# Rotating queries and keys with small transfers in place of a matrix product, on VectorE in another order

## The reference

```
h = modulate(x, norm_mix_g[l], shift1, scale1)      # shifts and scales from c_act @ w_ada + b_ada
proj = h @ w_in[l]                                  # pooled input, q, k, v, gates
q = rope_partial(qkv[0], pos)
k = rope_partial(qkv[1], pos)
attn = moba_attention(q, k, qkv[2])                 # 8 heads of 64
x = x + gate1 * (merged @ w_out[l])
x = x + gate2 * peer_ffn(modulate(x, ...), ...)     # 16 experts for each of 8 heads, by top-k

def rope_partial(x, pos):                           # half = 8 features
    x1, x2, rest = x[..., :half], x[..., half:16], x[..., 16:]
    return concatenate([x1 * cos - x2 * sin, x1 * sin + x2 * cos, rest], axis=-1)
```

## Time and profile before

| what | value |
|---|---|
| median of 3 runs | 1173.78 us (1173.57 to 1175.6) |
| the profiled execution | 1174.26 us, of which the span is 1172.4 us |
| PE busy | 1041.2 us, 89% |
| DVE busy | 826.7 us, 71% |
| ACT busy | 423.2 us, 36% |
| POOL busy | 290.3 us, 25% |
| chain that ended last | PE 52%, DMA 31%, DVE 11%, ACT 3% of the span |

### The profile page before, as it was taken

One profiled execution on the slowest core, in us unless ns is written; L12 is line 12 of the kernel. 1 busy time (PEld: TensorE's weight loads), 2 busy tenths in 40 slices (PEclk: granted clock), 3 DMA queues, 4 the chain that ended last, 5 costly groups with the idle time before them and its releaser, 6 DMA issues.

```text
span 1172.4 us, 13740 instructions
## 1 busy us (share of the span) xinstructions
PE 1041.2 (89%) x5066; PEld 702.4 (60%) x5066; DVE 826.7 (71%) x1912; ACT 423.2 (36%) x895; POOL 290.3 (25%) x262
## 2 busy tenths in 40 slices
PE   5999999898999996886886878788899999999997
PEld 3799976644555543432332323333389878999986
DVE  5699765768767768778887555555566878888843
ACT  3545622322332222222222111111266665665631
POOL 0000001444354543353544444445000000000000
PEclk8999999999999998898988999989999999999999
DMA  9977594999999999899999999999994443554530
GB/s 367 427 319 297 239 399 158 418 401 422 420 419 420 421 422 421 365 410 421 422 421 421 422 421 422 420 422 422 384 396 180 145 179 134 198 209 163 197 144 37
DMA packets 48199, 390.46 MB, mean 333 GB/s; under 512 B 5498, under 2 KB 5890, under 8 KB 7300
## 3 DMA queue, kind: packets, MB, share of 16 engines
q0 software_dynamic: 37040, 269.51, 55.5%
q1 hardware_dynamic: 11092, 120.07, 26.1%
HBM read 388.50 MB, written 1.06 MB: 332 GB/s over the span
## 4 chain that ended last, share of the span: by engine, by line
PE 52%; DMA 31%; DVE 11%; ACT 3%; issue 2%; POOL 1%; SPq 1%; DVEq 0%
DMA ring<-in_uv,idx 27%; PE ps L1457 18%; PE ps L1801 15%; PE ps L1958 5%; DMA ring<-in_w_ada 4%; DVE ring L1243 3%; PE ps L1669 2%; PE ps L1611 2%; PE ps L1886 2%; PE ps L1481 1%; PE ps L1684 1%; DVE ring_r L885 1%; POOL ring L514 1%; PE ps L1510 1%; DVE ring L896 1%
## 5 line engine op out<-in xcount | busy, mean ns | idle before, releaser
L1801 PE MATMUL ps<-ring,probT 128*128 128x512 f32 x1020 | 490.7, 625 | 103.6 <-ACT probT L759 102.1
L1243 DVE CUSTOM_DVE_ANT_0 ring<-h2t,ring 128x1024 f32<-128x1024 f32 x255 | 308.7, 1222 | 166.0 <-DMA ring<-in_uv,idx 165.8
L1801 PEld LDWEIGHTS ps<-ring,probT 128*128 128x128 f32 x1020 | 192.6, 199 | 338.8 <-issue 194.7
L514 POOL DMA_INDIRECT ring<-in_uv,idx x255 | 287.9, 1129 | 339.1 <-PE ps L1801 287.0
L1457 PE MATMUL ps<-util_r,ring_r 128*128 128x256 f32 x1312 | 216.9, 282 | 0.0
L1457 PEld LDWEIGHTS ps<-util_r,ring_r 128*128 128x128 f32 x1312 | 181.6, 189 | 1.3 <-issue 1.1
L885 DVE TENSOR_TENSOR ring_r<-ring,ring_r 128x1024 fp32r<-128x1024 f32 x134 | 157.7, 1220 | 34.0 <-ACT ring_r L536 33.9
L754 ACT ACTIVATE prob<-prob 128x2 f32<-128x2 f32 (+2 forms) x98 | 20.0, 204 | 368.5 <-DVE prob L1243 368.4
L536 ACT ACTIVATE ring_r<-ring 128x1024 fp32r<-128x1024 f32 x134 | 133.6, 1050 | 41.5 <-DMA ring<-in_w_in 19.3
L1457 PE MATMUL ps<-h_r,ring_r 128*128 128x256 f32 x704 | 126.1, 282 | 0.1
L759 ACT ACTIVATE probT<-ct,prob 128x128 f32<-128x128 f32 x256 | 85.5, 392 | 76.5 <-DVE prob L1249 75.8
(11 more groups left out here) (213 smaller groups left out, 980.4 us busy)
## 6 DMA issues: line engine op xcount, KB each, us to landing
ring<-in_w_in SPq DMA_DIRECT2D x12, 2048.0 KB, 13.8
ring<-in_w_up SPq DMA_DIRECT2D x11, 2048.0 KB, 7.9
ring<-in_w_ada SPq DMA_DIRECT2D x7, 2048.0 KB, 9.8
ring<-in_w_down SPq DMA_DIRECT2D x6, 2048.0 KB, 7.7
ring<-in_w_ada SPq DMA_DIRECT2D x8, 1024.0 KB, 16.4
ring<-in_w_out SPq DMA_DIRECT2D x4, 2048.0 KB, 8.0
ring<-in_w_q SPq DMA_DIRECT2D x3, 2048.0 KB, 11.3
ring<-in_w_br SPq DMA_DIRECT2D x2, 2048.0 KB, 13.1
```

Of the source, the lines that this page charges most:

```text
L514: e.indirect_dma_start(out=row_buf[n], out_offset=None, in_=uv, in_offset=bass.IndirectOffsetOnAxis(ap=idx[:, tt, k:k + 1], axis=0)).then_inc(
L1243: e.tensor_tensor_reduce(u, h2t[:, tt, :], u, 1.0, 0.0, ALU.mult, ALU.add, av[:, tt, n % 128:n % 128 + 1]).then_inc(*made.put(("dot", n)))
L1801: ins = e.matmul(acc[half][:, :], diag[:, n % 8, :], row_buf[n][:, D + half * 512:D + (half + 1) * 512], start=(k == 0), stop=(k == 127))
```

## The change

The matrix product goes. Instead GpSimd clears both scratch tiles, and as soon as ScalarE has copied all of the queries it issues four transfers within SBUF, each of 8 partitions x 1024 elements (32 KB), from `qT` into the scratch tile, with the groups of partitions exchanged. For the keys it does the same after their copy. VectorE's first pass now multiplies the scratch tile by `sinm` in place, whose sign moves from `rot` into the constant. The partitions that no transfer writes stay zero.

On VectorE the order of calls changes. The low parts of quarters 12 to 15 and `ada(6)` come ahead of the queries' rotation, the keys' rotation comes ahead of quarters 18 and 19, and `ada(5)` moves behind `normed` of heads 0 and 1, where `ada(7)` follows it directly. The order of the loads on SyncE is as it was.

```diff
--- before.py
+++ after.py
@@ -360,13 +360,15 @@
         arrived_in = {b: Mark(sem(f"s_rows{b[0]}{b[1]}"), 16) for b in bufs}
         arrived = [arrived_in[b] for b, _ in ROW_BUFS]
         spread_sums = Mark(sem("s_sums"), 16)
+        swapped = {name: Mark(sem(f"s_swapped_{name}"), 16) for name in ("q", "k")}
+        cleared = Mark(sem("s_cleared"))
         stored = Mark(sem("s_stored"), 16)
         high = Mark(sem("s_high"))
         low = Mark(sem("s_low"))
         done = Mark(sem("s_pe"))
         acted = Mark(sem("s_act"))
         made = Mark(sem("s_dve"))
-        marks = [*loaded, *half_loaded.values(), *once.values(), *arrived_in.values(), spread_sums, stored, high, low, done, acted, made]
+        marks = [*loaded, *half_loaded.values(), *once.values(), *arrived_in.values(), spread_sums, *swapped.values(), cleared, stored, high, low, done, acted, made]
         where = {}
 
         def bank(name):
@@ -496,6 +498,23 @@
         def gpsimd(e):
             pool = Engine(e)
 
+            pool.wait_ge(acted, ("row squares", 1, 1, 1))
+            for name in ("q", "k"):
+                e.memset(rope_of[name][1], 0.0).then_inc(*cleared.put(name))
+
+            def swap(name):
+
+                x3, scratch = rope_of[name]
+                pool.wait_ge(cleared, name)
+                for h in (0, 64):
+                    for a, b in ((h, h + 8), (h + 8, h)):
+                        e.dma_start(scratch[a:a + 8], x3[b:b + 8]).then_inc(*swapped[name].put((a, b)))
+
+            pool.wait_ge(acted, unit("in", 1, 2))
+            swap("q")
+            pool.wait_ge(acted, unit("in", 2, 2))
+            swap("k")
+
             for n in range(256):
                 tt, k = divmod(n, 128)
                 b, had = ROW_BUFS[n]
@@ -912,9 +931,9 @@
                 x3, scratch = rope_of[name]
                 for j0 in (0, 2):
                     xs, ss = x3[:, j0:j0 + 2, :], scratch[:, j0:j0 + 2, :]
-                    dve.wait_ge(done, ("rope", name, j0))
+                    dve.wait_ge(swapped[name], (72, 64))
                     dve.wait_ge(once["ct2"], 0)
-                    e.tensor_tensor(ss, pair(("rope", name, j0)), K("sinm").unsqueeze(1).broadcast_to([P, 2, T]),
+                    e.tensor_tensor(ss, ss, K("sinm").unsqueeze(1).broadcast_to([P, 2, T]),
                                     ALU.mult).then_inc(*made.put(("sin", name, j0)))
                     e.tensor_tensor(xs, xs, K("cosm").unsqueeze(1).broadcast_to([P, 2, T]), ALU.mult).then_inc(
                         *made.put(("cos", name, j0)))
@@ -1030,14 +1049,12 @@
                 x_low(1, h_sb, hi_r, k)
             split_low(*range(4, 12))
             ada(4)
-            split_low(12, 13)
+            split_low(*range(12, 16))
+            ada(6)
             rope("q")
-            split_low(14, 15)
-            ada(6)
             split_low(16, 17)
-            ada(5)
+            rope("k")
             split_low(18, 19)
-            rope("k")
             def modulation2():
 
                 dve.wait_ge(made, ("ada", 10, 3))
@@ -1054,6 +1071,8 @@
                 split_low(20 + 2 * s, 21 + 2 * s)
                 normed(1, 2 * s)
                 normed(1, 2 * s + 1)
+                if s == 0:
+                    ada(5)
                 if s in (0, 2):
                     ada(7 + s // 2)
             attended(1, 5)
@@ -1490,15 +1509,6 @@
                     for tt in tiles:
                         banks.give(("tokens", i, tt), acted if kind == "in" else made, ("v", i, tt))
 
-            def rope(name):
-                x3, _ = rope_of[name]
-                for j0 in (0, 2):
-                    o = group(("rope", name, j0))
-                    for jj in range(2):
-                        ins = e.matmul(o[:, jj * T:(jj + 1) * T], K("rot"), x3[:, j0 + jj, :], start=True, stop=True)
-                    ins.then_inc(*done.put(("rope", name, j0)))
-                    banks.give(("rope", name, j0), made, ("sin", name, j0))
-
             def pair_scores(att, i):
 
                 q3, k3, _, _, h = head_of(att, i)
@@ -1588,12 +1598,10 @@
             columns("in", 1, 2, xs, lambda k: [], acted)
             columns("in", 2, 0, xs, lambda k: [], acted)
             pe.wait_ge(acted, unit("in", 1, 2))
-            rope("q")
             columns("in", 2, 2, xs, lambda k: [], acted)
             tokens("in", 3, 0, xs, lambda k: [])
             pe.wait_ge(acted, unit("in", 2, 0))
             pe.wait_ge(acted, unit("in", 2, 2))
-            rope("k")
             tokens("in", 3, 2, xs, lambda k: [])
             columns("in", 4, 0, xs, lambda k: [], acted)
             pe.wait_ge(made, ("roped", "q", 0))
@@ -2019,7 +2027,7 @@
     for h in (0, 64):
         for m in range(8):
             cosm[h + m], cosm[h + 8 + m] = cos[m], cos[m]
-            sinm[h + m], sinm[h + 8 + m] = sin[m], sin[m]
+            sinm[h + m], sinm[h + 8 + m] = -sin[m], sin[m]
             rot[h + 8 + m, h + m] = -1.0
             rot[h + m, h + 8 + m] = 1.0
     put("cosm", cosm)
```

## The result

| | before | changed |
|---|---|---|
| median | 1173.76 us (1173.57 to 1175.6, 4 runs) | 1188.6 us (1186.98 to 1189.28, 4 runs) |
| ratio | 1 | 1.0121, interval 1.0103 to 1.0138 |
| profiled span | 1172.4 us | 1187.0 us |

The account below looks back on a forecast made before the run. VectorE and TensorE both reach the first scores at 85 us, then TensorE bounds the chain to 202.6. A 7.6 us stall plus 2.4 us of slow clock gave 10.0 us more: 1183.8 us, range 1179 to 1188.

Parts of the forecast that it names:

- The deciding term: VectorE at `ada 7`: its load, issued only at 92.4 us, leaves VectorE idle 7.7 us and starts `pair_values` 7.6 us later.
- the keys' landing: Ahead of the keys' rotation: transfers issued by 73.3 us, wanted at 76.2, taken to cost nothing; upper end 4.7 us late.
- the predicted 0.7 us for the scores: VectorE, done with quarters 18 and 19 at 82.3 us, waits for scores ending at 83.0, adding 0.7 us before `ada 5` ends.
- rival 2: Keys' transfers land late: with the tail of `in 5`, +1.5 us (1185.3); at the upper end +4.0 (1187.8); chance 0.16.
- The clause on the queries: Ahead of the queries' rotation: copied at 53.9 us, landed by 69.1 even at the slowest, wanted at 70.1, so covered.
- the 76.1 us: TensorE ahead of the scores: without 3.1 us of `rot` products the last columns could start at 76.1 in place of 79.16.
- The clock: TensorE behind its idle time of about 10.8 us: granted clock falls to half, costing 2.4 us.
- Rival 1: After TensorE's stall the clock doesn't fall, or TensorE isn't bound while it is low: 1181.4 us; chance 0.12.
- Rival 3: Later in the stage, where loads or ScalarE had been waited for, half of the 7.6 us is recovered: 1180.0 us; chance 0.08.
- Rival 4: The load of `ada 7` is no obstacle and TensorE's saved 3.1 us remain: 1170.7 us; chance 0.04.
- my upper end: Top of the forecast range for the whole kernel's median time: 1188 us.

Follow-up runs that it names:

- The experiment: 14 products added in TensorE's stall, against the changed kernel with the keys copied early (ratio 1.0100): 1185.07 us, ratio 1.0110 to the kernel before.

## Why the prediction came out as it did

**The deciding term was right.** The two chunks in one slot, the load issued only when the first is done, 7.6 us to its landing (7.67 measured), VectorE idle for 7.7 us (7.73), and ScalarE and TensorE behind it: each step stands in the trace, and putting `ada 5` back removes the whole loss. The issue came at 95.4 and not 92.4.

**What was mis-sized: the keys' landing.** "I take nothing, because the queue is nearly empty from 75 us" is the step that failed. The last transfer landed 6.2 us after its issue, and VectorE waited 4.27 us. With `ada 4` 0.7 us sooner and the predicted 0.7 us for the scores gone, the end of `ada 5` came 3.0 us later than I had it, and so did `pair_values` (10.7 in place of 7.6 us late). The low share of the DMA engines misled me. It is a mean over 16, and a low mean doesn't say that the load has landed: in the changed kernel it was 0.41 from 77 to 78 us and 0.14 from 78 to 79, and ScalarE got the load at 79.54. The earlier trace rows had shown the like, with the load there at 78.4. That was rival 2 with its tail of 1.5 us, but the tail lay 1.2 us later (79.5), since `in 4` and `in 5` came later in this run. The clause on the queries, that they were covered, was right for the new order alone.

**A wait that I overlooked.** TensorE's wait for ScalarE's copy of the keys had served the product with `rot`. It stands in the program without it and takes 1.42 us ahead of 71.87, because that copy is queued behind a weight load on ScalarE. Here the keys' transfers covered it. With these out of the way it would have bound: with the load held back, the keys had landed by 75.6 and the scores still started only at 84.66. So the 76.1 us at which I had the last columns start left out this wait. They started at 77.55.

**The clock** cost 2.3 us (2.4 predicted), read from the first stretch after the stall. That the size fits is in part luck, since it was taken from eight products of another shape. Rival 1 falls with it. The experiment gives 1.7 of it back in the trace, not 2.3, since ScalarE is close behind, and no gain is seen in its measured time.

**Rival 3**, that some is given back later, fell: 12.9 us late at 116.7 and at 212 us alike. **Rival 4** fell too. **The remaining 2.2 us** up to 220 us are the unnamed wait, of which I had no notion. Its cause stays open. The 14.6 us by which the profiled span grew are then the 10.0 of the forecast, 3.0 for the keys and 2.2 for that wait, less 0.6 us that the rest of the span came out shorter. The median of 1188.6 lies 0.6 us above my upper end.

## What to carry to other kernels

When work moves later on an engine, ask what buffer it frees, which load waits for that, and what is queued behind that load's user. Two users of one slot side by side expose a whole load, and here that cost more than the products taken away could give. A small transfer issued while 2 MB loads are in flight isn't small: the last of four landed 6 to 9 us after its issue here, so issue it that much ahead of its use. An engine's saved time is worth something only where it was the last to arrive: here VectorE arrived with TensorE. And work taken off TensorE can open an idle time behind which its clock is low: with the old order that took 1.5 us.

## What the runs showed of the hardware

- A transfer of 32 KB within SBUF lands in 2.0 us with no load in flight, and in 4.3 to 7.9 us (medians of four) with 2 MB loads in flight, by GpSimd's queue. The last of four took 6.2 us for the keys in the changed kernel and 9.2 us for the queries with the old order. By ScalarE's queue the last of four landed 5.8 us after its issue.
- Issues of such transfers took about 0.5 us each on GpSimd (2.05 to 2.21 us for four) and 0.8 us on ScalarE (3.21 us for four).
- In the unnamed wait at the start of the gathers, ScalarE stood still for 2.1 us and VectorE for 1.6 us beside it. It came in some profiles and not in others, which at 0.2% of the time is as much as the order of this stage can win.
- TensorE's granted clock was 0.50 behind 11.75 us of idle time in the changed kernel, and also behind 3.64 us with the old order and 2.62 us with `ada 5` put back. It stayed at 1.00 behind the 1.42 us in the changed kernel.
